# A hybrid decoder step: input loaded with channels on the partitions, block rows on GpSimd, gathers released behind the last states

## The reference

```
u = rmsnorm(h, norm_mix)                 # h * rsqrt(mean(h*h) + eps) * gain, per token
z, xbc, dt = split(u @ w_in)             # 2048, 4096 and 32 columns
xbc = silu(causal_conv(xbc, state_conv)) # 4 taps along the tokens, per channel
xs, bm, cm = split(xbc)                  # values, and B and C rows of 8 groups
dt = softplus(dt + dt_bias)
y, state = ssd_scan(xs, dt, -exp(a_log), bm, cm, state_ssm)
y = (y + d_skip * xs) * silu(z)          # grouped rmsnorm, then
h = h + norm(y) @ w_out
...
q = rmsnorm(h, norm_ffn) @ w_query       # PEER: 8 heads, top 16 of 128 x 128 sub-keys
act = gelu(u . expert_u[idx]);  h = h + sum(gate * act * expert_v[idx])
```

## Time and profile before

| | |
|---|---|
| median of 3 runs | 2444.46 us (2441.75 to 2446.61) |
| profiled execution | 2444.89 us, span 2443.1 us |
| TensorE | 1741.4 us busy, 71% of the span, mean granted clock 0.83 |
| VectorE | 1569.0 us, 64% |
| ScalarE | 260.7 us, 11% |
| GpSimd | 1340.1 us, 55% |
| gathers (software queue) | 671.17 MB, 67.9% of the DMA engines' span |
| direct DMAs | 186.46 MB, 20.3% |

### The profile page before, as it was taken

How to read it: one execution, slowest core, us unless ns; L and a number is a source line. 1 busy time by engine, 2 the same in 40 slices (tenths; PEclk the granted TensorE clock), 3 DMA queues, 4 the chain that set the end, 5 groups by cost and what they waited for, 6 DMA issues and landing times.

```text
span 2443.1 us, 22858 instructions
## 1 busy us (share of the span) xinstructions
PE 1741.4 (71%) x7437; PEld 762.4 (31%) x7437; DVE 1569.0 (64%) x3812; ACT 260.7 (11%) x628; POOL 1340.1 (55%) x1496
## 2 busy tenths in 40 slices
PE   7999799494406666678788676886756767556678
PEld 4577658334400010022335223451213412001112
DVE  2388777999798757652644898878765644733321
ACT  2133212001000000011110111110011100000000
POOL 0011653266547777755665556665645664677774
PEclk9999899596756666689889887787877978699999
DMA  4332257399979999999999999999999999999997
GB/s 162 111 131 70 94 181 257 119 407 417 417 268 407 420 420 419 420 409 416 416 419 416 413 415 364 419 416 417 416 414 420 408 415 386 396 419 420 419 419 294
DMA packets 270247, 859.09 MB, mean 352 GB/s; under 512 B 26288, under 2 KB 31344, under 8 KB 270128
## 3 DMA queue, kind: packets, MB, share of 16 engines
q0 software_dynamic: 184320, 671.17, 67.9%
q1 hardware_dynamic: 85808, 186.46, 20.3%
HBM read 845.26 MB, written 12.17 MB: 351 GB/s over the span
## 4 chain that ended last, share of the span: by engine, by line
POOL 23%; DMA 18%; PE 11%; issue 9%; DVE 8%; ACT 0%; SPq 0%; POOLq 0%; DVEq 0%; ACTq 0%
POOL arena L2491 23%; DMA arena<-peer_v,arena 11%; PE banks L880 4%; DVE arena L2137 3%; PE banks L1072 3%; DMA wring<-w_q 2%; DMA arena<-peer_u,arena 2%; DMA wring<-ple_w_gate 1%; DMA wring<-peer_w_query 1%; PE banks L820 1%; DMA wring<-w_o 1%; PE banks L989 1%; DVE arena L1951 1%; PE banks L558 1%; DVE arena L1948 1%
## 5 line engine op out<-in xcount | busy, mean ns | idle before, releaser
L2137 DVE SCALAR_TENSOR_TENSOR arena<-arena,banks 128x1024 f32<-128x1024 f32 x640 | 763.1, 1219 | 451.5 <-DMA arena<-peer_u,arena 445.1
L1072 PE MATMUL banks<-arena 128*32 128x512 f32 x2560 | 703.5, 726 | 383.3 <-DMA arena<-peer_v,arena 376.9
L2491 POOL DMA_INDIRECT arena<-peer_u,arena x640 | 606.2, 947 | 386.2 <-issue 186.4
L2491 POOL DMA_INDIRECT arena<-peer_v,arena x640 | 607.4, 949 | 351.1 <-issue 173.4
L1072 PEld LDWEIGHTS banks<-arena 128*32 128x32 f32 x2560 | 93.7, 117 | 870.3 <-DMA arena<-peer_v,arena 704.9
L880 PE MATMUL banks<-wring,uT 128*128 128x512 f32 (+3 forms) x448 | 217.5, 634 | 40.7 <-DMA wring<-w_q 17.8
L558 PE MATMUL banks<-cst,arena 128*128 128x128 f32 (+2 forms) x349 | 61.3, 330 | 147.3 <-DVE arena L2153 82.2
L634 PE MATMUL banks<-uT,wring 128*128 128x320 f32 x512 | 139.1, 433 | 0.0
L880 PEld LDWEIGHTS banks<-wring,uT 128*128 128x128 f32 (+1 forms) x448 | 78.0, 184 | 188.2 <-issue 153.5
L2424 POOL COPY arena<-arena 128x3 f32<-128x3 f32 x32 | 6.0, 188 | 207.5 <-ACT arena L1416 207.5
L634 PEld LDWEIGHTS banks<-uT,wring 128*128 128x128 f32 x512 | 96.7, 190 | 39.8 <-issue 0.4
(11 more groups left out here) (270 smaller groups left out, 1883.2 us busy)
## 6 DMA issues: line engine op xcount, KB each, us to landing
wring<-peer_w_query SPq DMA_DIRECT2D x40, 1024.0 KB, 18.4
wring<-ssm_w_in SPq DMA_DIRECT2D x24, 1024.0 KB, 7.2
wring<-w_q SPq DMA_DIRECT2D x18, 1024.0 KB, 20.4
wring<-ssm_w_out SPq DMA_DIRECT2D x16, 1024.0 KB, 9.1
wring<-ple_w_gate SPq DMA_DIRECT2D x12, 1024.0 KB, 12.2
arena<-peer_u,arena POOLq DMA_INDIRECT x640, 11.6
arena<-peer_v,arena POOLq DMA_INDIRECT x640, 9.9
out_sample_ssm<-arena SPq DMA_DIRECT2D x16, 512.0 KB, 3.8
```

What stands on the lines that cost most here:

```text
L1072: mm = pe.matmul(sums(t, at, half), place_of(t, at), rows_buf[:, k, half * 512:(half + 1) * 512], start=at < spots(t), stop=False, skip_gr ...
L2137: dve.scalar_tensor_tensor(rows_buf[:, k, :], rows_buf[:, k, :], 1.0, u_now, ALU.mult, ALU.mult, accum_out=pact[:, n % 2, at:at + 1]).then ...
L2491: pool.indirect_dma_start(rows_buf[:, k, :], None, tables[kind], bass.IndirectOffsetOnAxis(ap=rows, axis=0))\
```

## The change

Four parts are changed together.

1. The input is also given transposed (`x_T`, channels on the partitions, and `gain_T`), and loaded straight into `uT`. VectorE multiplies it by the gain in place, in two halves. The factor 1/rms of the tokens, which no longer is in `uT`, is applied where the products are read: as ScalarE's scale of the tanh and VectorE's factor in the gate (`half_rstd`), in dt's first step (`rstd`), and as a row over the tokens in the convolution stage (`rstd_row`, which TensorE makes out of ones times a diagonal). The norm's multiplication, the 24 transposes and ScalarE's copies of them go. z block 0 now stands ahead of dt, and SyncE's issues are put into another order.
2. In the convolution stage VectorE reads the PSUM block itself (`take_block`) and multiplies it by the row; ScalarE's two copies go.
3. The block rows of the samples' scan are made by GpSimd (8 instructions of 128x512) in place of VectorE.
4. The token `scan_over` is passed behind the last `new_states`, ahead of `turn_rows(2)`. GpSimd also waits for ScalarE's last squares there.

The core of the diff:

```diff
@@ TensorE
+            gate_block(0)
             pe.wait_ge(*cst_in.at("cst"))
-            norm_transposes("mix0")
+            pe.wait_ge(*dve_done.at("rstd_diag"))
+            acc = claim(pe, "rstd_row")
+            for t in range(3):
+                mm = pe.matmul(acc[:, OFF[t]:OFF[t] + ROWS[t]], ones[0:ROWS[t], :], rstd_diag[0:ROWS[t], t, 0:ROWS[t]],
+                               start=True, stop=True)
...
-            gate_block(0)
...
-                pe.wait_ge(*dve_done.at(("bm", g)))
+                pe.wait_ge(*pool_done.at(("bm", g)))
@@ SyncE
+            sp.dma_start(uT[:, 0:4, :], I["x_T"][:, 0:4, :]).then_inc(x_in[0].sem, 16)
+            sp.wait_ge(*dve_done.at("small"))
+            sp.dma_start(gainT, I["gain_T"]).then_inc(gainT_in.sem, 16)
+            load_weights(sp, 1)
+            sp.dma_start(uT[:, 4:8, :], I["x_T"][:, 4:8, :]).then_inc(x_in[1].sem, 16)
+            load_weights(sp, 2)
...
-            load_weights(sp, 2)
+            load_weights(sp, 4)
@@ ScalarE
-                        s(act.activation(z[:, t, n * 512:(n + 1) * 512], bank, ACT.Tanh, scale=0.5), act_done, ("ztanh", n, t))
+                        s(act.activation(z[:, t, n * 512:(n + 1) * 512], bank, ACT.Tanh, scale=half_rstd[:, t:t + 1]),
+                          act_done, ("ztanh", n, t))
...
-                s(act.activation(raw[:, b % 4, 3:259], bank[:, 0:256], ACT.Copy))
-                freeing(act.activation(raw[:, b % 4, 259:347].rearrange("p (b w) -> p b w", b=8)[:, :, 3:11],
-                                       bank[:, 256:320].rearrange("p (b w) -> p b w", b=8), ACT.Copy), ("xbc", b))
@@ VectorE
+            for half in range(2):
+                dve.wait_ge(x_in[half].sem, 16)
+                part = uT[:, 4 * half:4 * half + 4, :]
+                s(dve.tensor_tensor(part, part, spread(gainT[:, 4 * half:4 * half + 4], NTOK), ALU.mult), dve_done, ("input", half))
...
+            def take_block(b):
+                bank = filled(dve, ("xbc", b))
+                dve.wait_ge(*pool_done.at(("rawstate", b)))
+                s(dve.tensor_tensor(raw[:, b % 4, 3:259], bank[:, 0:256], rstd_row[:, 0:256], ALU.mult))
+                of_seq = lambda v: v.rearrange("p (b w) -> p b w", b=8)
+                freeing(dve.tensor_tensor(of_seq(raw[:, b % 4, 259:347])[:, :, 3:11], of_seq(bank[:, 256:320]),
+                                          of_seq(rstd_row[:, 256:320]), ALU.mult), ("xbc", b))
...
-                if n == 2 * GROUPS - 1:
-                    block_rows(0)
-                if t == 2 and g + 1 < GROUPS:
-                    block_rows(g + 1)
...
                 if t == 2:
                     new_states(g)
+                    if g == GROUPS - 1:
+                        tell("scan_over")
...
             turn_rows(2)
-            tell("scan_over")
@@ GpSimd
+                    pool.wait_ge(*freed("ec"))
+                    s(pool.tensor_tensor(bm[:, g % 2, :, :], repeat(btok[:, 2, g * 128:(g + 1) * 128], 4),
+                                         spread(cst[:, C_SEQ:C_SEQ + 4], 128), ALU.mult), pool_done, ("bm", g))
...
             pool.wait_ge(*dve_done.at("scan_over"))
+            pool.wait_ge(*act_done.at(("gsq", 2, GROUPS - 1)))
```

More of the change, by code:

```diff
@@ L463, in build @@
         rows_in = signal("conv_rows_loaded")
+        x_in = [signal(f"turned_input_loaded{i}") for i in range(2)]
+        gainT_in = signal("turned_gain_loaded")
         dtw_in = signal("dt_weights_loaded")
@@ L594, in gate_block @@
                 for half in range(2):
+                    if n == 0:
+                        pe.wait_ge(*dve_done.at(("input", half)))
                     w = weight(pe, ("z", n, half), ("z", n, 2))
@@ L1224, in store_state @@
                              hnew[:, blk % 2, :, :]).then_inc(*hnew_out[blk % 2].mark(blk, 16))
-            for t in range(3):
-                for half in range(2):
-                    sp.wait_ge(*full_at(("uT", "mix0", t, half)))
+            sp.wait_ge(*squares.at(("mix0", 2)))
             def load_state(blk):
@@ L1381, in norm @@
                     take_turned(key, t)
-            norm("mix0", lambda t: h_in[t].at("x"))
+            for t in ALL:
+                square("mix0", t, h_in[t].at("x"))
+            bank = filled(act, "rstd_row")
+            freeing(act.activation(rstd_row, bank[:, 0:NTOK], ACT.Copy), "rstd_row")
             act.wait_ge(vec_in.sem, 48)
@@ L1397, in _ @@
                             s(act.activation(z[0:64, 2, n * 512 + 256 * c:n * 512 + 256 * c + 256],
-                                             bank[64 * c:64 * c + 64, 0:256], ACT.Tanh, scale=0.5), act_done, ("ztanh", n, 2))
+                                             bank[64 * c:64 * c + 64, 0:256], ACT.Tanh, scale=half_rstd[64 * c:64 * c + 64, 2:3]),
+                              act_done, ("ztanh", n, 2))
             def conv_tanh(b):
@@ L1821, in _, with gate @@
             s(dve.memset(small[:, :], 0.0), dve_done, "small")
-            norm("mix0", 0)
+            dve.wait_ge(gainT_in.sem, 16)
+            for half in range(2):
+                dve.wait_ge(x_in[half].sem, 16)
+                part = uT[:, 4 * half:4 * half + 4, :]
+                s(dve.tensor_tensor(part, part, spread(gainT[:, 4 * half:4 * half + 4], NTOK), ALU.mult), dve_done, ("input", half))
+            dve.wait_ge(*squares.at(("mix0", 2)))
+            s(dve.tensor_scalar(var[:, 0:3], ssq[:, 0:3], 1.0 / D, EPS, ALU.mult, ALU.add))
+            rsqrt(rstd[:, 0:3], var[:, 0:3], nwt[:, 0:3])
+            s(dve.tensor_copy(rstd[64:128, 2:3], rstd[0:64, 2:3]))
+            s(dve.tensor_scalar(half_rstd, rstd[:, 0:3], 0.5, None, ALU.mult), dve_done, "half_rstd")
+            dve.wait_ge(*cst_in.at("cst"))
+            for t in range(3):
+                s(dve.tensor_scalar(rstd_diag[:, t, :], ident, rstd[:, t:t + 1], None, ALU.mult),
+                  *((dve_done, "rstd_diag") if t == 2 else ()))
+            def gate(n):
+                for t in range(3):
+                    zz = z[0:ROWS[t], t, n * 512:(n + 1) * 512]
+                    dve.wait_ge(*act_done.at(("ztanh", n, t)))
+                    s(dve.tensor_scalar(zz, zz, 1.0, half_rstd[0:ROWS[t], t:t + 1], ALU.add, ALU.mult))
+                    bank = filled(dve, ("z", n, t))
+                    if t < 2:
+                        freeing(dve.tensor_tensor(zz, zz, bank, ALU.mult), ("z", n, t))
+                    else:
+                        s(dve.tensor_tensor(zz[:, 0:256], zz[:, 0:256], bank[0:64, 0:256], ALU.mult))
+                        freeing(dve.tensor_tensor(zz[:, 256:512], zz[:, 256:512], bank[64:128, 0:256], ALU.mult), ("z", n, t))
             dve.wait_ge(vec_in.sem, 48)
@@ L1826, in _ @@
                 bank = filled(dve, ("dt", t))
-                freeing(dve.tensor_tensor(dt[:, t, :], bank[:, 0:32], dtb_bc, ALU.add), ("dt", t))
+                freeing(dve.scalar_tensor_tensor(dt[:, t, :], bank[:, 0:32], rstd[:, t:t + 1], dtb_bc, ALU.mult, ALU.add), ("dt", t))
             s(dve.scalar_tensor_tensor(dtmp, dt, -1.0, dt, ALU.mult, ALU.max), dve_done, "dt_abs")
@@ L1840, in _ @@
             for n in range(4):
[L1841 to L1850, removed]
+                gate(n)
+            def take_block(b):
[5 more added lines that the diff above has]
+                                          of_seq(rstd_row[:, 256:320]), ALU.mult), ("xbc", b))
             def conv(b):
-                dve.wait_ge(*freed(("xbc", b)))
+                take_block(b)
                 if b >= 3:
@@ L1877, in _ @@
             dve.wait_ge(rows_in.sem, 32)
+            dve.wait_ge(*freed("rstd_row"))
             for b in range(CONV_BLKS):
@@ L2003, in after_sample_turn @@
                     advance(early_picks, (3, 3, 2, 2, 2)[g - 3])
[L2005 to L2012, removed]
             def new_states(g):
```

13 lines of the change are left out of this document (8 added, 5 removed).

## The result

The changed kernel takes 2453.2 us (median of 20 runs, 2447.84 to 2457.88) against 2445.57 of the kernel before (20 runs). The ratio is 1.0031, 95% interval 1.0024 to 1.0039: 7.6 us slower, 5.9 to 9.5. I had forecast 2443.0, no measurable change, with 2433 to 2452 as the range. The profiled execution took 2449.66 us (span 2447.9).

The account below looks back on a forecast made before the run. TensorE, with VectorE close behind, was taken to bound the kernel before the gathers, DMA after them. Front and convolution +9.4, block rows −2.7 and early gathers −8.2 summed to −1.5: 2443.0 us, no measurable change, range 2433 to 2452.

Parts of the forecast that it names:

- Front: Norm, z blocks and dt up to the convolution stage: that stage starts 2.8 us earlier (−5 to +1).
- z block 0's start: First z matmuls no longer wait for norm, transposes and dt: start near 8.0 us, 20.2 earlier (−21 to −17).
- the bank wait: TensorE stands ahead of z block 1 until VectorE's gate products free PSUM banks: +8.1 us (0 to 10).
- rival 2: Front: the wait for banks ahead of z block 1 costs little, 6 to 8 us go: 2436 us; chance 0.10.
- The slow restart: TensorE runs at half pace after standing ahead of z block 1: +2.2 us (0 to 4).
- Convolution stage: VectorE becomes the bound at 4.98 us per block against TensorE's 4.57: +12.2 us.
- Rival 1: Convolution stays TensorE-bound, VectorE's block under 4.57 us, the stage keeps 146.4: 2431 us; chance 0.17.
- rival 3: Convolution: VectorE's new steps are dearer, block 5.3 us, stage +22.4: 2453 us; chance 0.18.
- Block rows: Samples' scan: eight multiplications leave VectorE for GpSimd, −2.7 us (−3.5 to +1).
- Early token: Gathers released right behind the last state: first gather 8.2 us sooner and the lead stays, −8.2 (−3.4 to −9).
- rival 4: Gathers: VectorE bounds their first phase, so only 3.4 us of the early release counts: 2448 us; chance 0.10.
- The sign that I had set for it: VectorE's waits for gathers vanish at 500 to 660 us while the end doesn't move.

Follow-up runs that it names:

- e2: Changed kernel with the token scan_over put back behind turn_rows(2), undoing the fourth part: 2453.36 us, ratio 1.0035 to the kernel before.
- e1: Kernel before with only the fourth part, scan_over passed behind the last states: 2440.23 us against 2445.18, ratio 0.9983.
- e4: Changed kernel with z block 0's tanh and gate moved ahead of dt's softplus on ScalarE and VectorE: 2442.55 us, ratio 0.9990 to the kernel before.

## Why the prediction was wrong, step by step

**Front: right in kind, 1.7 too good.** z block 0's start (8.0 forecast, 8.22), dt (6.0; 5.5) and the bank wait (8.1; 8.3) hold. The sum, −2.8, reads −3.3 on the profile I worked from, but that profile has the latest start of four executions of the same front (98.62 to 101.87, mean 100.2). Against this mean the changed kernels' 98.5 to 99.8 (four, mean 99.1) is −1.1. The stand is there, so rival 2 is out. The slow restart that I had priced at +2.2 behind it is there too, but belongs to dt (last section).

**Convolution stage: right.** VectorE became the bound, 4.93 per block where I had 4.98, and the stage is 11.2 longer where I had 12.2. Rival 1 is out, and so is rival 3: the steps took 0.42 and 0.22. By the errata table of the Trainium skill (page "VectorE: DVE Perf Modes", section on the TRN2 errata: 120 fixed cycles for a source in PSUM and one per element, at 0.96 GHz) they would take 0.39 and 0.19, an estimate; the trace has 0.03 more of each. The formula that the same section of the Trainium skill has for an fp32 tensor_tensor, (N + 151)/0.96 ns, given there for 512 and 2048 elements, makes 0.424 and 0.224 of 256 and 64, and with that the trace agrees.

**Block rows: wrong, −2.7 forecast, −0.2 measured over the whole scan, no gain to be told from none.** Of the steps at which I let VectorE's 0.69 count, the first does gain: from one sample step's states to the next 24.4 in place of 25.1 to 25.2, in all ten profiles. Of the six steps that follow, two gain some 0.4 each in the means (the fourth step takes 16.0 to 16.4 in place of 16.6 to 16.8, the sixth 15.1 in place of 15.5), and the others are level within 0.1 or 0.2 longer. From the first of the samples' states to the last that is 1.2 gained: 116.0 to 117.5 us with the rows on GpSimd (mean 116.5), 117.2 to 118.7 on VectorE (mean 117.8). But the stretch ahead, from the stage's end to the first of these states, is 1.0 longer in the mean with the rows on GpSimd (100.8 against 99.8). It varies from 98.3 to 101.0 among the executions with the rows on VectorE, so whether the rows cost it anything isn't shown. So I let too many steps count, and I had put GpSimd's interference at 0.5 in sum, where three pairs of one trace show 1.7.

**Early token: wrong, and the step that decides.** I wrote that VectorE waited 19.6 us for gathers and "has the time to catch up, so the lead stays: −8.2". The lead of the first gather was there (9.6 us against the last state, better than forecast), but VectorE was not waiting where it mattered. The 19.6 us in rows 8 lie at two places, as the waits above show: 4.6 at the first four dots and 15.0 behind 610 us. Between the two, for over 100 us, VectorE stands for nothing (49.00 of 50 in rows 1). That is the phase that a lead has to pass, and it lets through only what VectorE itself gained, 4.6. Of this some 2 more went to the hole in DMA. That was rival 4, whose price (−3.4) was between the two readings (−4.6 and −2.6); I gave it 0.10. The sign that I had set for it, that VectorE's waits for gathers vanish up to 660 us, was wrong: those behind 610 us remain (16.8 us in 24 waits in the changed kernel).

**The sum.** With the parts as measured, −1.1 + 11.2 − 0.2 − 2.6 = +7.3 against 7.6 (5.9 to 9.5) in the medians. My −1.5 missed by 5.6 in the token, 2.5 in the rows, 1.7 in the front, and 1.0 the other way in the stage. That the sum comes within 0.3 of the medians is in part luck: the front, the scan and the token are each known to about 1 us at best.

**What stays open.** Behind the 421st gather the traces drift for a reason that I have not found: the next 80 gathers take 120.5 us in the profile of before, 121.1 to 125.1 in the others, whichever change they have. So single profiles differ at the end by some 3 us more or less than at the 141st gather, and the token's worth in the changed kernel's median (none to be told by e2's times, 4.2 by e1's in the kernel before, 2.6 to 2.9 by the traces at the 141st gather) isn't settled by the times.

## What to carry to other kernels

A wait total over a long stretch doesn't say that an engine can catch up: split it, and look for the stretch between, in which it waits for nothing; a lead given ahead of such a stretch is worth only the waits ahead of it. A factor that has to be applied somewhere is cheapest where it is applied once (3 us on the input) and not at each of 32 readings (11 us), even when each reading needs only 0.7 us. A new claim in a ring of buffers waits for whoever frees the oldest, so what stands ahead of that freeing on its engine must be part of the sum.

## What the hardware did that I had not expected

TensorE's clock fell without a stand. In e4 TensorE is busy for all of these stretches, and the granted clock (the third column from the end) still drops while dt's 64 matmuls of 32 columns run (28.85 to 34.7):

```profile
28.00:32.00 4.00, 4.00 (x35) 3.81 (x35) 1.70 (x5) 1.61 (x4) 0.00 (x0) 1.00 0.70 221
32.00:36.00 4.00, 4.00 (x40) 3.36 (x40) 0.76 (x3) 0.50 (x2) 0.00 (x0) 0.52 0.80 306
36.00:40.00 4.00, 4.00 (x7) 1.49 (x7) 2.29 (x8) 1.35 (x2) 0.00 (x0) 0.62 0.00 2
40.00:44.00 4.00, 4.00 (x12) 1.57 (x12) 0.42 (x2) 0.00 (x0) 0.00 (x0) 1.00 0.00 0
```

0.52 is near the lower of the two levels (1.2 of 2.4 GHz, read as 0.5 and 1.0); seven large matmuls fit in the stretch from 36 to 40 where 12 fit in the next. In the changed kernel the clock falls in the same stretch, with dt's matmuls in it too:

```profile
32.00:36.00 4.00, 2.78 (x42) 2.61 (x41) 0.76 (x3) 0.45 (x2) 0.00 (x0) 0.64 0.88 338
```

A mean of 0.64 of two levels means that the clock was down from about 33.1 on, and the stand begins only at 34.8. So the 2.2 us that I had charged to the stand ahead of z block 1 remain when the stand goes, and dt's place among the z blocks is enough to bring them. What in dt's matmuls lets the clock fall, no run here separates.
